# Unread matmuls in PE's gaps, an earlier copy of the gate columns, and products with the higher part first

## What is computed

```
mod = silu(c) @ w_ada + b_ada            # 2048 x 12288, six parts
h = rmsnorm(x, g1) * (1 + sc1) + sh1
x = x + gt1 * mixer(h, ...)              # w_in; 4 mLSTM heads both ways, 8 attention heads; w_out
h = rmsnorm(x, g2) * (1 + sc2) + sh2
x = x + gt2 * ((silu(h @ w_gate) * (h @ w_up)) @ w_down)
return rmsnorm(x, g_final)
```

## Time and profile before

| | us |
|---|---|
| three runs | 2378.56, 2378.80, 2383.15 |
| median | 2378.8 |
| the profiled execution | 2378.83 |
| its span, first to last instruction | 2376.4 |
| PE busy in the span | 2274.8 |

### The profile page before, as it was taken

How to read it: one execution, slowest core, us unless ns; L and a number is a source line. 1 busy time by engine, 2 the same in 40 slices (tenths; PEclk the granted TensorE clock), 3 DMA queues, 4 the chain that set the end, 5 groups by cost and what they waited for, 6 DMA issues and landing times.

```text
span 2376.4 us, 27461 instructions
## 1 busy us (share of the span) xinstructions
PE 2274.8 (96%) x10500; PEld 1884.7 (79%) x10500; DVE 1520.4 (64%) x1732; ACT 892.2 (38%) x1041; POOL 231.6 (10%) x85
## 2 busy tenths in 40 slices
PE   5898999999998999899999999999999999999997
PEld 4777878788886788788888888888888888888886
DVE  6857565564657556667877887788778644444443
ACT  4333232223226411454444444444444434333332
POOL 0001333333420011100000000000000001010000
PEclk8898999999999999899999999999999999999999
DMA  9932444444452268314434443445344755454552
GB/s 360 374 122 91 157 142 144 170 146 142 168 201 74 107 244 316 124 62 169 166 133 141 140 169 132 141 137 172 132 141 135 297 210 198 178 206 182 190 199 107
DMA packets 188193, 405.27 MB, mean 171 GB/s; under 512 B 9280, under 2 KB 67920, under 8 KB 172496
## 3 DMA queue, kind: packets, MB, share of 16 engines
q1 hardware_dynamic: 175088, 388.01, 46.0%
q10 hardware_dynamic: 13024, 16.13, 1.9%
HBM read 384.19 MB, written 19.92 MB: 170 GB/s over the span
## 4 chain that ended last, share of the span: by engine, by line
PE 81%; DVE 11%; issue 4%; ACT 2%; DMA 1%; POOL 0%; DVEq 0%; SPq 0%; ACTq 0%; POOLq 0%
PE ps L1712 25%; PE ps L1714 24%; PE ps L1713 24%; DVE qk L1256 2%; PE ps L1844 1%; DVE acc L1286 1%; DMA araw<-in_w_ada 1%; DVE qk L1253 1%; PE ps L2115 1%; PE ps L1857 1%; PE ps L1855 1%; PE ps L1743 1%; PE ps L1956 1%; DVE acc L1053 1%; DVE u2b L1584 0%
## 5 line engine op out<-in xcount | busy, mean ns | idle before, releaser
L887 ACT ACTIVATE whi<-wraw 128x1024 fp32r<-128x1024 f32 x200 | 212.0, 1061 | 261.4 <-PE ps L1714 137.0
L1712 PE MATMUL ps<-h_hi,whi 128*128 128x512 f32 x720 | 291.8, 405 | 13.6 <-DVE h_lo L1082 13.6
L1544 DVE TENSOR_TENSOR wlo<-wraw,whi 128x1024 fp32r<-128x1024 f32 x200 | 240.5, 1219 | 76.7 <-ACT whi L887 76.7
L1714 PE MATMUL ps<-h_hi,wlo 128*128 128x512 f32 x720 | 285.3, 396 | 0.0
L1713 PE MATMUL ps<-h_lo,whi 128*128 128x512 f32 x720 | 285.3, 396 | 0.0
L1712 PE MATMUL ps<-d_hi,whi 128*128 128x512 f32 x704 | 274.3, 390 | 0.0
L1714 PE MATMUL ps<-d_hi,wlo 128*128 128x512 f32 x704 | 273.9, 389 | 0.0
L1713 PE MATMUL ps<-d_lo,whi 128*128 128x512 f32 x704 | 273.9, 389 | 0.0
L1653 DVE TENSOR_TENSOR d_lo<-d_raw,d_hi 128x2048 fp32r<-128x2048 f32 x44 | 100.8, 2291 | 244.1 <-ACT d_hi L952 244.1
L1712 PE MATMUL ps<-whi,sk_hi 128*128 128x512 f32 x640 | 251.8, 393 | 4.6 <-DVE u2b L1584 4.6
L1714 PE MATMUL ps<-whi,sk_lo 128*128 128x512 f32 x640 | 249.5, 390 | 0.0
(11 more groups left out here) (294 smaller groups left out, 3873.0 us busy)
## 6 DMA issues: line engine op xcount, KB each, us to landing
araw<-in_w_ada SPq DMA_DIRECT2D x64, 1024.0 KB, 5.6
wraw<-in_w_gate SPq DMA_DIRECT2D x88, 512.0 KB, 3.8
wraw<-in_w_up SPq DMA_DIRECT2D x88, 512.0 KB, 4.7
d_raw<-aT_keep SPq DMA_DIRECT2D x44, 1024.0 KB, 4.8
wraw<-in_w_down SPq DMA_DIRECT2D x44, 1024.0 KB, 7.1
wraw<-in_w_in SPq DMA_DIRECT2D x39, 1024.0 KB, 5.3
acc<-in_w_up SPq DMA_DIRECT2D x40, 512.0 KB, 5.5
wraw<-in_w_out SPq DMA_DIRECT2D x16, 1024.0 KB, 8.2
```

What stands on the lines that cost most here:

```text
L887: A(EHI[e % 4], src, ACT.Copy).then_inc(uhi_ok, 1)
L1544: V_.tensor_tensor(ELO[e % 4], src, EHI[e % 4].bitcast(F32), ALU.subtract).then_inc(ulo_ok, 1)
L1712: pe.matmul(o, w_hi, m_hi, start=first, stop=False)
L1714: return pe.matmul(o, w_lo, m_hi, start=False, stop=last)
```

## The change

`keep_busy` is new: `times` matmuls of `mask3` (384 columns) against `ones`, plain float32, into a bank whose content nobody reads. It is called behind the columns of each quarter (three matmuls, bank 4) and, ahead of the feed-forward part, behind `sum_columns(1)` (three, bank 6) and behind the spread of the roots (five, bank 6). In the first tile of each quarter's products, and in the first unit of the feed-forward part, PE waits for the higher part alone, makes the two matmuls that read it for all six or eight banks, then waits for the lower part and makes the third. DVE copies `acol` ahead of the angles; ACT calls `trig_tables` in head 1 behind the exponentials of j = 1.

```diff
@@ ACT, first() and body()
-                trig_tables()
                 exp_minus_m()
                 turned_v(0)
...
                     if j < 4 and mixing:
                         exps(m, j, m * 4)
+                    if j == 1 and isinstance(h, int) and h == 1:
+                        trig_tables()
@@ DVE
             conv_pair(0, 2)
+            gate_columns()
             trig()
             trig_round(2048.0)
             trig_round(1.0)
             trig_end()
-            gate_columns()
@@ PE, front_slot()
+                    first = k == 0 and s % 2 == 0
+                    if first:
+                        pe.wait_ge(hhi_ok, kt + 1)
+                        for t in range(6):
+                            c0 = k * FCOLS + t * P
+                            for w in (whi, wlo):
+                                pe.matmul(ps[FBANK[t]][:], w[s % 2][:, c0:c0 + P], h_hi[:, kt, :],
+                                          start=kt == 0 and w is whi, stop=False)
                     pe.wait_ge(hlo_ok, kt + 1)
                     for t in range(6):
                         c0 = k * FCOLS + t * P
-                        last = mm3(...)
+                        if first:
+                            pe.matmul(ps[FBANK[t]][:], whi[s % 2][:, c0:c0 + P], h_lo[:, kt, :], start=False, stop=False)
+                        else:
+                            last = mm3(...)
@@ PE
+            def keep_busy(bank=4, times=3):
+
+                for _ in range(times):
+                    pe.matmul(ps[bank][:, 0:3 * P], ones[:], mask3[:], start=True, stop=True)
...
             ada_columns(0)
+            keep_busy()
             for quarter in range(1, 4):
                 front_slot(2 * quarter - 2)
                 front_slot(2 * quarter - 1, quarter)
                 ada_columns(quarter)
+                keep_busy()
...
             sum_columns(1)
+            keep_busy(6)
             pe.wait_ge(modp_ok, 12)
             pe.wait_ge(n_dg, 1)
             for tb in range(TB):
                 last = pe.matmul(ps[7][:, tb * P:(tb + 1) * P], ones[:], sqt[:, 0, tb * P:(tb + 1) * P], start=True, stop=True)
             last.then_inc(n_bc, 1)
+            keep_busy(6, 5)
@@ PE, first unit of the feed-forward part, k == 0 and i == 0
+                    if first:
+                        pe.wait_ge(fhi_ok, 1)
+                        for t in range(TB):
+                            hi = (q1_hi, A21[0])[t // 2]
+                            for g in range(2):
+                                for b in (b_hi, b_lo):
+                                    pe.matmul(ps[4 * g + t][:], hi[:, 0, t % 2 * P:t % 2 * P + P], b[:, g, :],
+                                              start=b is b_hi, stop=False)
                     pe.wait_ge(flo_ok, 2 * k + i + 1)
...
+                            if first:
+                                pe.matmul(ps[4 * g + t][:], lo[:, 0, part], b_hi[:, g, :], start=False, stop=False)
+                                continue
```

5 lines of the change are left out of this document (3 added, 2 removed).

## The result

The changed kernel takes 2361.37 us (median of 4 runs, 2359.47 to 2363.44) against 2378.68 for the kernel before, timed beside it: a ratio of 0.9923, 95% interval 0.9906 to 0.994. The ratio is one of means (the medians alone give 0.9927). The profiled execution took 2361.09 us, its span is 2359.3; before it was 2378.83 and 2376.4. So the working can be set against the spans, which differ by 17.1 us; another 0.6 us went outside them.

What follows compares the result with a forecast made beforehand. PE, busy for 96% of the span, was taken as the bound, losing idle time and half clock. Front 4.0, gate 6.3 and feed-forward 1.5 sum to 11.8 us: 2378.8 to 2367.0 us, range 2361.0 to 2373.0 for 8 in 10.

Steps and rivals of the forecast that it cites:

- Gate columns ahead of the angles: Gate stretch: DVE copies `acol` before the angles, so PE goes on 6.3 us earlier; ends 5.0 and 11.6.
- Its cover: Gate edit: late angles on DVE and ACT's delayed hi(15) cost nothing, covered by PE slots of 10.5 us.
- I leave its half clock as it is: Chain behind the gate columns: half clock taken as unchanged; 5.3 us more if the clock stayed up.
- The front: adaLN quarters and the transition behind the last columns: together 4.0 us, low end 2.0, high end 5.2.
- the three inner transitions: Between the adaLN quarters: PE's rows offer 7.2 us, but DMA takes all but 2.2.
- The signs listed for a wrong step: Among them: last columns of the front well before 124.5, L2066 over 1.5 us behind `sqt`, new half clock behind 228.
- The last transition: Behind the last adaLN columns, free of the DMA limit: 1.8 us gained, ends 0.3 and 2.9.
- The order of the products: adaLN quarters: higher part first lets products start up to 1.1 us earlier in one transition, with h_lo covered.
- Ahead of the feed-forward part: Unread matmuls and higher part first bring products to full clock: 1.5 us gained, ends 2.4 and -1.5.
- the first rival: The clock never falls in the three places edited: 2359.6 us; chance 0.12.
- Unread matmuls buy nothing: They are late as much as they help, and only the copy of `acol` counts: 2372.5 us; chance 0.13.
- gate gain given back: Late angles on DVE or ACT's hi(15) cost the whole gate gain: 2373.3 us; chance 0.06.

Runs made afterwards that it cites:

- e1_gate: The kernel before with the gate edit alone (gate columns ahead of the angles, angle functions moved on ACT): 2372.28 us, ratio 0.9966.
- e2_front: The kernel before with only the unread matmuls and the higher-part-first order of products in the adaLN quarters: 2373.88 us, ratio 0.997.
- e10_light_both: The changed kernel with two of three products left out in quarter slots 0 to 5 and DVE adding only 512 of 1024 columns: 2366.78 us, ratio 0.9942.
- e4_no_three: The changed kernel without the three unread matmuls ahead of the spread of the roots: 2361.45 us.
- e5_front_first: The kernel before with only the higher-part products first in the adaLN quarters, no unread matmuls: 2379.06 us, ratio 0.9991.
- e11_gate_busy: The changed kernel without the three unread matmuls ahead of L2086, and with two behind the gate columns: 2361.62 us, ratio 0.9911.
- e6_front_busy: The kernel before with only three unread matmuls behind each of the four sets of columns, product order as before: 2373.63 us, ratio 0.9969.
- e9_tables_early: The changed kernel with the functions of the angles back in their old place on ACT: 2371.16 us, ratio 0.9964.
- e7_light_front: The changed kernel with two of three products left out in slots 0 to 5 of the adaLN quarters: 2366.89 us, ratio 0.994.
- e13_light_five: The changed kernel with two of three products left out in quarter slots 0 to 5, five unread matmuls ahead of the last three column sets: 2366.75 us, ratio 0.9937.
- e12_light_busy: The changed kernel with two of three products left out in quarter slots 0 to 5, eight unread matmuls ahead of the last three column sets: 2364.54 us.

## Why the prediction was too high, step by step

**Gate columns ahead of the angles** held to the hundredth: 7.08 less 0.78 is 6.30 us. Its cover held too. The angles end on DVE at 211.8 and `md` starts behind them, 2.0 us after ACT has copied `bc` (0.7 was said), within PE's slot; ACT's table load and three functions take 3.2 us (3.3 was said), and PE waits for no low part of POOL. "I leave its half clock as it is" is a term of the sum that was too small: 1.95 us came in the changed kernel, 0.4 in e1_gate. It was within the end of 11.6.

**The front** has the failed step: "the three inner transitions together are worth not the 7.2 that PE's rows offer but 2.2 us: DMA takes the rest". Measured: 4.2 in the changed kernel, 4.8 in e2_front. Two readings were wrong in it. First, PE being 2.0 to 2.2 us behind DVE was taken as one lag, to be won once. It is made anew in each quarter, because DVE waits in each for PE's columns: a cycle of 27.2 us against the 25.2 of DVE's chain (the first, with its columns at half clock, 28.8 against 26.9), so some 2.0 to win in each of three. Secondly, a DMA share of 1.05 with the queues empty from 122 was taken as a queue that could not be faster. From 110 to 120 us it moved 352 GB/s, and moved 373 as soon as DVE freed its buffers earlier. The bound was real but 2.5 us earlier than placed: 78.5 us from first to last columns in e10_light_both, where a gain of 2.2 meant 81.0. The signs listed for a wrong step came: last columns at 122.91, before 124.5. The 7.0 us of the whole front lie beyond the 5.2 of its stated high end, while the two other parts stayed within their ends. Beside this, of the 6.0 us that DVE's chain allowed, the first cycle gave only 0.8, its unread matmuls being at half clock, and the third 1.3, with the clock down at 100.0 to 103.4 and 0.74 us of waiting for a transfer; the second gave all of its 2.0.

**The last transition** was 2.7 us, not 1.8, with the clock up all through it. e2_front had 1.5 and e4_no_three 1.6, and in both the clock is down for 3.4 us from 125 on. The ends were 0.3 and 2.9: a term mis-sized within its range.

**The order of the products** was said to bring 1.1 us a transition. By e5_front_first it brings nothing at half clock, and with the unread matmuls nothing that can be told from the scatter, 0.7 us in all at most.

**Ahead of the feed-forward part**: 1.45 us against 1.5, which is luck, by terms that were both off. The three unread matmuls put 1.51 us on the path, the upper bound stated, not the 0.5 taken, and L2086 hardly shortened (1.91 against 2.04). In return the five behind it were not late, and the first product came 1.0 us sooner behind L2086, at full clock.

**The sum**: 3.0 us more in the front, 1.95 in the gate stretch, 0.5 in the middle and 0.6 outside the span, less 0.1 from the feed-forward part on, give the 5.9 us between 11.8 and 17.7 of the profiled executions. Of the 3.0 in the front 2.0 are the failed step; the clock of the gate stretch, 1.95, is as large, but its case was within that part's ends. The low end of the range kept the cap on the quarters and so left out the case that came.

**The rivals.** The clock still fell, at 205.8 and 963.5 and once in the quarters, with idle gaps of only 0.8, 1.1 and 0.6 us ahead:

```profile
100.00:103.40 3.40, 3.40 (x9) 2.07 (x8) 2.88 (x5) 3.40 (x5) 0.00 (x0) 0.53 1.05 386
...
963.50:970.40 6.90, 6.90 (x22) 5.08 (x23) 2.25 (x13) 0.67 (x1) 1.01 (x1) 0.52 0.23 95
```

These are windows of the changed kernel; the second begins within the short columns that start at 963.24. So the first rival is not what happened, though its 2359.6 lies nearer to the measured time than the forecast does. The rule of the Trainium skill, TensorE: Matmul & The Clock Gate, section Why this matters for your kernels, that closed gaps prevent the fall, holds here in part: of the three falls behind sets of columns one is left, at 100.0, while in e11_gate_busy the clock falls with no gap at all. "Unread matmuls buy nothing" is refuted by e6_front_busy, and "gate gain given back" by e1_gate; e9_tables_early shows what it would have looked like.

## What to carry to other kernels

When two engines wait for each other once per round, take each engine's own chain over one round (its time without the waits) and multiply the difference by the rounds; a lag read at the end of one round is not the whole reserve. Before a full DMA queue is taken as the bound, ask whether its transfers waited for buffers that the slow engine held: the waits of the issuing queue and the GB/s of the last stretch tell. And matmuls that come earlier but still at half clock were worth nothing here: fill the gap so that the clock is up first.

## What the runs showed of the hardware that was not expected

Less work on PE made the kernel slower. e7_light_front leaves out half of the products of the quarters and is 4.0 to 5.5 us slower than the changed kernel. 1.6 us of that are in the quarters, since the columns on the path then run at half clock (3.58 us instead of 1.84), and e13_light_five gets them back; 3.7 are behind the last columns, which run at half clock too.

Products that start earlier don't bring the clock back earlier. With the first product 1.0 us sooner behind the columns it came back 1.4 us later behind them (e5_front_first).

The clock also falls under a PE that never stands. Windows of the kernel before, at the end of a head, where 8 transposes and 16 one-column matmuls (the sums, L1743, 3.63 us) stand between the products:

```profile
530.00:535.70 5.70, 5.70 (x48) 5.40 (x47) 5.46 (x7) 2.43 (x2) 1.61 (x1) 1.00 0.75 285
535.70:539.10 3.40, 3.40 (x10) 2.65 (x9) 3.25 (x2) 0.00 (x0) 2.94 (x1) 0.52 0.00 0
```

PE has been busy without a break since 500 us, and the clock falls some 0.7 us after the sums have ended. It can also stay down under a busy PE. Windows of e12_light_busy, in slots with one matmul of 128x512 and two one-column matmuls (four records) in turn:

```profile
84.50:94.70 10.20, 10.20 (x37) 8.82 (x37) 9.51 (x8) 1.48 (x1) 0.00 (x0) 0.50 1.06 378
```

This stretch begins behind 1.28 us of idle time (81.4 to 82.7); all 10.2 us are busy, and all at half clock. In the changed kernel, whose slots have three of the large matmuls to the two one-column ones, the clock stays up from 103.4 to 205.8. And the same 670 us of code took 673.7 to 679.7 us from kernel to kernel, with a mean clock of 0.97 or 0.96: on this kernel an edit that is worth 2 us can be read in a milestone next to it, and hardly in the end time.
